# First two attentions of a two-block kernel: values stationary with two heads in column halves, probabilities normalised before they are transposed, four probability buffers

## The reference, cut to what matters

```
s_own = einsum('bhqd,bhkd->bhqk', qc, k_own) * scale        # attention A, 64 features
s_own = where(k_pos <= q_pos, s_own, -inf)
p = softmax(...);  y_a = einsum('bhqk,bhkd->bhqd', p, v)
s = einsum('bhqd,bhkd->bhqk', qb, k) * scale                # attention B, 96 features
p = softmax(where(k_pos <= q_pos, s, -inf));  y_b = einsum('bhqk,bhkd->bhqd', p, v)
merged = sigmoid(gate_a) * (y_a @ w_branch_a) + sigmoid(gate_b) * (y_b @ w_branch_b)
x = x + merged @ w_out
```

## Time and profile before

| | |
|---|---|
| median of 3 runs | 1720.45 us (1718.86 to 1721.94) |
| the profiled execution's own time | 1720.27 us |
| its span (first to last instruction) | 1718.4 us |
| PE busy | 1685.3 us, 98% of the span |
| DVE, ACT, POOL busy | 961.0, 902.1, 1023.5 us |
| the chain that ended last | PE 87%, DVE 4%, ACT 3%, POOL 2% |
| the two attentions | 86.71 to 142.41 us of the span |

### The profile page before, as it was taken

One profiled execution on the slowest core, in us unless ns is written; L12 is line 12 of the kernel. 1 busy time (PEld: TensorE's weight loads), 2 busy tenths in 40 slices (PEclk: granted clock), 3 DMA queues, 4 the chain that ended last, 5 costly groups with the idle time before them and its releaser, 6 DMA issues.

```text
span 1718.4 us, 29498 instructions
## 1 busy us (share of the span) xinstructions
PE 1685.3 (98%) x9320; PEld 1432.7 (83%) x9320; DVE 961.0 (56%) x2062; ACT 902.1 (52%) x1638; POOL 1023.5 (60%) x549
## 2 busy tenths in 40 slices
PE   8999999999999999999999989999999999999998
PEld 7887998888888888888888888888888877788887
DVE  6333489887778885555555557753222266532222
ACT  5565654445444445555445566525555665555554
POOL 4846768888777762000000068627888886578886
PEclk9999999999999999999999999999999999999999
DMA  6634545555544446555655645215555564255553
GB/s 225 177 97 133 203 158 183 183 187 183 166 160 155 157 157 193 191 192 193 195 193 190 224 138 158 74 50 165 187 191 188 179 179 140 85 179 195 186 193 123
DMA packets 83073, 288.18 MB, mean 168 GB/s; under 512 B 9264, under 2 KB 9264, under 8 KB 82480
## 3 DMA queue, kind: packets, MB, share of 16 engines
q1 hardware_dynamic: 82560, 286.10, 51.5%
q10 hardware_dynamic: 432, 1.05, 0.2%
HBM read 285.01 MB, written 2.10 MB: 167 GB/s over the span
## 4 chain that ended last, share of the span: by engine, by line
PE 87%; DVE 4%; ACT 3%; POOL 2%; issue 2%; DMA 1%; DVEq 0%; ACTq 0%; POOLq 0%; SPq 0%
PE acc L652 13%; PE col L955 13%; PE acc L653 13%; PE acc L654 13%; PE col L1249 7%; PE col L957 7%; PE col L1253 4%; POOL w_lo L2022 2%; PE col L689 1%; PE col L690 1%; PE col L691 1%; PE mb L969 1%; PE acc L1168 1%; PE mb L970 1%; ACT w_hi L1465 1%
## 5 line engine op out<-in xcount | busy, mean ns | idle before, releaser
L2022 POOL TENSOR_TENSOR w_lo<-w_raw,w_hi 128x1024 fp32r<-128x1024 f32 (+1 forms) x403 | 952.9, 2380 | 296.7 <-ACT w_hi L1465 274.4
L1465 ACT ACTIVATE w_hi<-w_raw 128x1024 fp32r<-128x1024 f32 (+1 forms) x539 | 565.5, 1052 | 292.1 <-PE acc L654 233.0
L955 PE MATMUL col<-hT,w_hi 128*128 128x512 f32 x1024 | 365.2, 401 | 0.0
L957 PE MATMUL col<-hT,w_lo 128*128 128x256 f32 x1024 | 287.0, 280 | 0.0
L955 PEld LDWEIGHTS col<-hT,w_hi 128*128 128x128 f32 x1024 | 192.4, 188 | 45.7
L652 PE MATMUL acc<-w_hi,W_hi 128*128 128x512 f32 x512 | 199.4, 389 | 0.4 <-ACT W_hi L1686 0.2
L653 PE MATMUL acc<-w_lo,W_hi 128*128 128x512 f32 x512 | 199.2, 389 | 0.0
L654 PE MATMUL acc<-w_hi,W_lo 128*128 128x512 f32 x512 | 199.2, 389 | 0.0
L957 PEld LDWEIGHTS col<-hT,w_lo 128*128 128x128 f32 x1024 | 193.5, 189 | 0.0
L2064 POOL TENSOR_SCALAR_AFFINE_SELECT WST<-WST 128x512 f32<-128x512 f32 x1 | 1.1, 1116 | 319.4 <-DMA WST<-in_gmlp_w 319.4
L2747 DVE TENSOR_TENSOR w_lo<-w_raw,w_hi 128x1024 fp32r<-128x1024 f32 x128 | 156.2, 1221 | 1.3 <-ACT w_hi L1465 1.3
(11 more groups left out here) (589 smaller groups left out, 3070.7 us busy)
## 6 DMA issues: line engine op xcount, KB each, us to landing
w_raw<-in_expert_u SPq DMA_DIRECT2D x128, 512.0 KB, 3.3
w_raw<-in_expert_v SPq DMA_DIRECT2D x128, 512.0 KB, 4.3
w_raw<-in_w_mlp SPq DMA_DIRECT2D x128, 512.0 KB, 3.3
w_raw<-in_w_in SPq DMA_DIRECT2D x24, 512.0 KB, 3.9
w_raw<-in_w_qkv_o SPq DMA_DIRECT2D x24, 512.0 KB, 4.0
w_raw<-in_w_query SPq DMA_DIRECT2D x16, 512.0 KB, 3.3
w_raw<-in_w_gate SPq DMA_DIRECT2D x16, 512.0 KB, 3.4
w_raw<-in_w_qkv_e SPq DMA_DIRECT2D x12, 512.0 KB, 3.8
```

Source lines behind the costliest of these rows:

```text
L955: mm(both, wh[:, k, :], hT[:, :, k, :], start=k == 0, stop=k == KD - 1, skip_group_check=True)
L957: m = mm(both[:, 0, :], wl[:, k, :], hT_hi[:, k, :], start=False, stop=k == KD - 1, skip_group_check=True)
L1465: f(w_hi[:, s, 0:w], w_raw[:, s, 0:w], ACT.Copy).then_inc(sem(f"hi{s}"), 1)
L2022: g.tensor_tensor(w_lo[:, s, 0:w], w_raw[:, s, 0:w], w_hi[:, s, 0:w].bitcast(F32), ALU.subtract).then_inc(sem(f"lo{s}"), 1)
```

## The change

- Values: V of a head (128 tokens x 64 features) is stationary and the transposed probabilities move, 256 columns for key block 0 and 128 for key block 1. Two heads make a pair: the even head writes partitions 0 to 63 of a bank, the odd head 64 to 127. A pair's values are computed in the even turns. The result is features x tokens, so `Y`, `branch_out` and all `y_map` transposes go.
- Normalisation: DVE multiplies `Pr` by the reciprocal of the sums before the transposes (`normed`), one `tensor_tensor` product per query block for each head. PE's transposes wait for it ("probs") where they waited for ACT's exponential.
- `PT` has two buffers of two heads each, instead of one.
- A heads' scores go in pairs, the two heads' matmuls alternating, in the even turns.
- The high and low parts are taken by ACT (`heads_hi`) and DVE (`heads_lo`) straight from `acc[b]`, two pairs at a time; those of B have buffers of their own (`yB_hi`, `yB_lo`).
- The first chunk of br_a waits for its banks one by one. ACT splits gate_b's chunks 2 and 3 a turn or two later than before.

```diff
-        PT = big("PT", 86, [P, 2, 3 * P])
-        Y = big("Y", 90, [P, 2, NT, 8, 64])
+        PT = [big("PT0", 86, [P, 2, 3 * P]), big("PT1_", 106, [P, 2, 3 * P])]
...
-            def scores(u):
-                if u >= 2:
-                    pe.wait_ge(sem("masked"), u - 1)
...
+            def scores(*units):
+                for u in units:
+                    if u >= 2:
+                        pe.wait_ge(sem("masked"), u - 1)
+                    if u >= A_H and u % 2 == 0:
+                        pe.wait_ge(sem("qb_E"), upto("qb_E", u - A_H + 2))
+                for u in units:
+                    q, k = qk_of(u)
+                    mm(col[u % 2][:, 0:P], q[:, 0:P], k[:, 0:P], start=True, stop=True)
+                for u in units:
+                    q, k = qk_of(u)
+                    mm(col[u % 2][:, P:3 * P], q[:, P:2 * P], k, start=True, stop=True).then_inc(
+                        sem("scores"), 1)
...
-            def head_values(u):
...
+            def pair_values(p):
+                b, kk = p % 4 // 2, p % 2
+                pe.wait_ge(sem("pT_E"), upto("pT_E", 2 * p + 2))
+                if p == 0:
+                    pe.wait_ge(sem("ev_kvup"), upto("ev_kvup", 2))
+                if p >= 4 and kk == 0:
+                    pe.wait_ge(sem("yA_E"), b + 1)
+                for kt in range(NT):
+                    for hh in range(2):
+                        h = 2 * p % 8 + hh
+                        v = VC[:, kt, h * 64:(h + 1) * 64] if p < 4 else VB[:, kt, h, :]
+                        o = acc[b][64 * hh:64 * hh + 64, kk * SEQ + kt * P:(kk + 1) * SEQ]
+                        pt = PT[p % 2][:, hh, 0:2 * P] if kt == 0 else PT[p % 2][:, hh, 2 * P:3 * P]
+                        m = mm(o, v, pt, start=kt == 0, stop=kt == 1, skip_group_check=True)
+                m.then_inc(sem("pv"), 1)
...
             for u in range(A_H + B_H):
-                pe.wait_ge(sem("exp"), u + 1)
+                pe.wait_ge(sem("probs"), u + 1)
                 if 5 <= u <= 12:
                     pe.wait_ge(sem("qb_E"), upto("qb_E", u - 4))
-                if 13 <= u <= 14:
-                    pe.wait_ge(sem("yA_E"), upto("yA_E", u - 12))
                 causal_fills(u, Pr[:, u % 2, :], "pT", "pT_E")
-                if u + 2 < A_H + B_H:
+                if u + 2 < A_H:
+                    if u % 2 == 0:
+                        scores(u + 2, u + 3)
+                elif u + 2 < A_H + B_H:
                     scores(u + 2)
-                if u:
-                    head_values(u - 1)
+                if u and u % 2 == 0:
+                    pair_values(u // 2 - 1)
                 if 4 <= u <= 11:
+                    pe.wait_ge(sem("pT_E"), upto("pT_E", u))
                     b_map(u)
-                if 12 <= u <= 13:
-                    y_map(0, u - 12, mb[(u + 1) % 2], "yA_T")
                 gate_b(u)
-            head_values(A_H + B_H - 1)
+            pair_values(A_H - 1)
+            def after_gate_b(t, n):
+                if t:
+                    pe.wait_ge(sem("ev_gb"), upto("ev_gb", 3 + n))
+                else:
+                    pe.wait_ge(sem("yB_E"), n + 1)
...
-                if n >= 2:
-                    act.wait_ge(sem(free), upto(free, n - 1))
-                f(dst[:, n % 2, :], mb[n % 2][:, 0:3 * P], ACT.Copy).then_inc(sem(signal), 1)
+                if n >= 4:
+                    act.wait_ge(sem(free), n // 2 - 1)
+                f(dst[n // 2 % 2][:, n % 2, :], mb[n % 2][:, 0:3 * P], ACT.Copy).then_inc(sem(signal), 1)
+            def heads_hi(m, b, name, pairs):
+                act.wait_ge(sem("pv"), pairs)
+                f(m[:, 2 * b:2 * b + 2, :].rearrange("p k s -> p (k s)"), acc[b][:, :],
+                  ACT.Copy).then_inc(sem(name), 1)
...
-                if u == 1:
-                    split_to(FIRST["gb"] + 4)
+                if u in (1, 2):
+                    split_to(FIRST["gb"] + 1 + u)
...
+                if u in (5, 9):
+                    heads_hi(yA_hi, (u - 5) // 4, "yA_H", (u - 1) // 2)
+                if u == 13:
+                    heads_hi(yB_hi, 0, "yB_H", 6)
             copy_probs(0, PT, "pT", "pv", A_H + B_H - 1, "pT_E")
             gate_b(1)
+            heads_hi(yB_hi, 1, "yB_H", 8)
             split_to(FIRST["br_a"] + 4)
-            stream_hi("y", range(2))
...
+            def normed(u):
+                dve.wait_ge(sem("exp"), u + 1)
+                then(v.reciprocal(sums[:, u, :], sums[:, u, :]))
+                for t, (a, b) in enumerate(((0, P), (P, 3 * P))):
+                    p = Pr[:, u % 2, a:b]
+                    i = v.tensor_tensor(p, p, sums[:, u, t:t + 1].to_broadcast([P, b - a]), ALU.mult)
+                    if t == 0:
+                        go(i)
+                i.then_inc(sem("probs"), 1)
...
                 masked(Sm[:, u % 2, :], col[u % 2], causal, mx[:, u, :], "masked")
+                if u:
+                    normed(u - 1)
...
+                if u in (8, 12):
+                    heads_lo(yA_hi, yA_lo, (u - 8) // 4, "yA_H", "yA_E")
+            normed(A_H + B_H - 1)
+            for b in range(2):
+                heads_lo(yB_hi, yB_lo, b, "yB_H", "yB_E")
```

More of the change, by code:

```diff
@@ L352, in program @@
         QTA = big("QTA", 40, [P, 8, SEQ])
[L353 to L354 removed]
+        yB_hi = big("yB_hi", 40, [P, 4, SEQ], F32R)
+        yB_lo = big("yB_lo", 44, [P, 4, SEQ], F32R)
         QB = big("QB", 48, [P, NT, B_H, B_DK])
@@ L645, in row_chunk @@
                         second_half()
-                    if t == 0 and n == 0 and t0_freed:
-                        pe.wait_ge(sem(t0_freed[0]), upto(*t0_freed))
+                    if bank_free:
+                        bank_free(t, n)
                     a, b = splits_of(j)[n]
@@ L821, in b_map @@
                 m.then_inc(sem("qb_T"), 1)
[L823 to L831, removed]
             def gate_b(u):
@@ L854, in gate_b @@
                     m.then_inc(sem(f"used{s}"), 1)
-            scores(0)
-            scores(1)
+            scores(0, 1)
             row_group("kvup", "ev_qup", *from_c(2))
             for u in range(A_H + B_H):
-                pe.wait_ge(sem("exp"), u + 1)
+                pe.wait_ge(sem("probs"), u + 1)
                 if 5 <= u <= 12:
                     pe.wait_ge(sem("qb_E"), upto("qb_E", u - 4))
-                if 13 <= u <= 14:
-                    pe.wait_ge(sem("yA_E"), upto("yA_E", u - 12))
@@ L873, in _ @@
                     b_map(u)
-                if 12 <= u <= 13:
-                    y_map(0, u - 12, mb[(u + 1) % 2], "yA_T")
                 gate_b(u)
-            head_values(A_H + B_H - 1)
[L880 to L886, removed]
-            for k in range(4):
[L888 to L894, removed]
+            pair_values(A_H - 1)
@@ L895, in _, with of @@
+            def after_gate_b(t, n):
[3 more added lines that the diff above has]
+                    pe.wait_ge(sem("yB_E"), n + 1)
+            def of(m):
+                return lambda k: lambda t: m[:, k, t * P:(t + 1) * P]
+            pe.wait_ge(sem("yA_E"), 2)
+            for k in range(4):
+                row_chunk(FIRST["br_a"] + k, 0, of(yA_hi)(k), of(yA_lo)(k), k == 0, k == 3,
                           order=(1, 0) if k == 0 else range(NT),
-                          t0_freed=("y", 4) if k == 0 else None)
@@ L2424, in masked, with heads_lo @@
                 i.then_inc(sem(name), 1)
-            def branch_out(br):
-                dve.wait_ge(sem("exp"), 8 * br + 8)
-                then(v.reciprocal(sums[:, 8 * br:8 * br + 8, :], sums[:, 8 * br:8 * br + 8, :]))
-                dve.wait_ge(sem("pv"), 8 * br + 8)
-                for t in range(NT):
-                    then(v.tensor_tensor(Y[:, br, t, :, :],
-                                         acc[t][:, :].rearrange("p (h d) -> p h d", h=8),
-                                         over(sums[:, 8 * br:8 * br + 8, t], [P, 8, 64], 2),
-                                         ALU.mult), "y")
+            def normed(u):
[7 more added lines that the diff above has]
+                i.then_inc(sem("probs"), 1)
+            def heads_lo(hi, lo, b, name, done):
+                dve.wait_ge(sem(name), upto(name, b + 1))
+                k = slice(2 * b, 2 * b + 2)
+                v.tensor_tensor(lo[:, k, :].rearrange("p k s -> p (k s)"), acc[b][:, :],
+                                hi[:, k, :].bitcast(F32).rearrange("p k s -> p (k s)"),
+                                ALU.subtract).then_inc(sem(done), 1)
             dve.wait_ge(sem("causal"), 3)
```

46 lines of the change are left out of this document (9 added, 37 removed).

## The result

| | median (range), us | against before |
|---|---|---|
| before | 1719.57 (1718.86 to 1721.94, 11 runs) | |
| after | 1725.03 (1722.59 to 1727.47, 11 runs) | 1.0031, 95% interval 1.0022 to 1.0039 |
| predicted | 1713.0 (1710.6 to 1718.6) | |

The changed kernel is slower by 0.31%, 5.5 us, where 7.4 us less were forecast. The forecast started from 1720.45, a median of 3 runs; from the 1719.57 of 11 runs, 7.4 less is 1712.2. The rival that had the smallest chance has come true: DVE's products are held by POOL.

What follows compares the result with a forecast made beforehand. PE was taken to bound the kernel (busy 98% of the span). PE work 9.03 less, plus 0.80 for Y's transposes, minus 2.4 of new waits, made 7.4 less: from 1720.45 to 1713.0, range 1710.6 to 1718.6.

Steps and rivals of the forecast that it cites:

- the third rival: DVE's normalising products stand until POOL's low parts end: 11 us held in all, kernel slower at 1724; chance 0.06.
- the two held lines of the earlier trace: DVE instructions L2410 and L3141, held by POOL's w_lo: 2.51 beside 0.32 usual, 2.19 beside 0.22.
- the point of decision: Held DVE products decide the outcome from 7.4 us on, seven of the ten.
- Ten low parts at 1.1 each: In the two attentions, each POOL low part holds one head's product for 1.1 on average: 11 us.
- The pieces on PE: PE's transposes, scores, values, map and gate_b over the two attentions: sum 46.67 against 55.70 before, 9.03 less.
- serial halves: Values' column halves run one after the other, 1.53 a pair instead of 0.87: gain 2.1, time 1718.3; chance 0.15.
- the rule of the Trainium skill: On PE, a weight load overlaps running matmuls only if the row group differs; value pairs would go towards the serial price.
- The new waits: PE waits for DVE's new step: 0.59 in each of turns 7, 9, 11, 0.29 in turn 14, 0.3 at the start; 2.4.
- The late chain: Exponential, product, evacuation late in nearly every turn; turn 3's margin 0.07; 0.3 a head costs 4.8: 1717.8; chance 0.11.
- the tail behind the loop: After the loop, heads_hi and heads_lo end about 2.0 after the last values; covered by br_a's first chunk within 0.2.
- the 0.80 of the Y maps: Behind the two attentions, the 8 transposes of Y of B, about 0.1 each, go: 0.80 less.

## Why the prediction was wrong

- **The step that failed** is the argument against the third rival: "L2747 is a plain two-source product, all SBUF, beside POOL's w_lo, 1219 in the median and 1319 at most over 128 times", and from it "The held ones are of two other operations". The row is right, the words "beside POOL's w_lo" are not. L2747 is DVE's share of the low parts, at 646 to 990 us, and POOL has none there, as a window of the kernel before with the w_lo tiles alone shows:

```profile
core 0: us, POOL busy (x), PEclk, DMA share, GB/s
646.00:990.00 344.00, 0.00 (x0) 1.00 0.60 197
```

  So 128 unhurried products proved nothing, and the two held lines of the earlier trace rows, which did lie beside low parts, were set aside as exceptions. The rival had the mechanism, the place and the point of decision (7.4 us held); it got a chance of 0.06 on this reading. The other one against it, the reciprocal L3140, is right but says nothing of a product: reciprocals weren't held here either (0.16 inside a low part), products were.
- **Its size.** Ten low parts at 1.1 each made 11 us, and 1724. Measured: seven heads at 2.05 on average, 14.4 us, and 0.4 by `rope_t` on head 0; 1725.03. Fewer heads and more a head than I had: in five of the seven the product and a low part start within 0.4 us of one another. Not all reaches PE (13.6 us of waits, 11.2 beyond the 2.4 forecast). That 1724 comes so near is partly luck.
- **The pieces on PE** held. A pair of values takes 0.80 (forecast 0.87) whichever way it is queued, a pair of scores 0.86 (0.87). The serial halves (1.53) didn't come about, so the rule of the Trainium skill that the prediction set against it (TensorE: Matmul & The Clock Gate, The mechanism: loads overlap only if the row group differs) did not show here: both heads' loads fill the same rows, and the pair takes 0.80, near the 0.66 that the prediction's sum has for one head's columns and far from the 1.32 for two.
- **The new waits** apart from the hold: 2.4 forecast, 2.0 measured with the low parts cut, counted from start to start. They are 0.46, 0.55 and 0.45 before turns 8, 10 and 12 (0.59 each), 0.30 before turn 1 (0.3) and 0.25 before turn 14 (0.29). The profile's brackets show 0.28 to 0.39 for the first three and nothing for the others. One term was missing: the first transposes come 0.34 later (87.05 for 86.71), ahead of this sum, behind head 0's product that `rope_t` holds.
- **The late chain** in turn 3 and the tail behind the loop: neither appears. With the holds gone or mostly gone the stretch is 48.93 to 50.37 in four kernels, 49.07 forecast. Their medians, 1712.5 to 1713.3, are 6.4 to 7.2 under the kernel before that ran beside each (7.4 forecast).
- **After the stretch**: the 0.80 of the Y maps came (22.69 for 23.60). The profile of the changed kernel also has 3.4 us at the lower clock level behind the merge (granted clock 0.94 from 170.44 to 199.00, matmuls 0.43 apart instead of 0.23), which cost it 1.6. PE had stood idle for 0.62 and 0.98 us shortly before; the kernel with the squared product has the same two idles and kept its clock. From 170.44 to its end it takes 1552.9, where the kernel before takes 1552.4 from the same place, so 4.4 of the 4.9 us that its span is longer had come before the fall. The two kernels with the product in another form have the same holds and a clock of 1.00 there, and their spans are 1722.1 and 1722.0 for 1723.3. So that fall doesn't belong to every execution and isn't the cause of the loss; whether it has a share in the median of the changed kernel stays open.

## What to carry to other kernels

Before an instruction is put on DVE beside POOL's long ones, look where its operands lie: with all of them in SBUF it can stand until the POOL instruction ends, with an input in PSUM it did not. If such a step lies on the path, start POOL's work behind it (here one wait, 7 us, and 12 with the product moved ahead of the mask) or move that work; how often they meet isn't given by POOL's share of time, since both may be released by the same engine. And a row that is to prove that two things don't disturb each other proves it only if both ran at that time: open the window of the second engine first.

## What the runs showed of the hardware

- A held product ends just behind the POOL instruction, 0.15 us for 128 columns and 0.28 for 256, whenever it began: 128 columns of 0.29 took 0.71 to 2.44 in the changed kernel, 256 columns of 0.42 took 2.59 and 2.60. A reciprocal of 128x2 inside the same low parts stayed at 0.16.
- The reverse is small: low parts that start together with a product take 2.52 to 2.53 instead of 2.37 to 2.39, and a POOL instruction of 0.73 beside head 0's second product takes 1.00.
- Two heads in the column halves run together in either queueing order: 0.80 and 0.81 for a pair of 2 x (256 + 128) columns in fp32.
- A wait added to POOL made the kernel 7.1 us faster: in neither profile does PE wait for one of the low parts from 84 to 250 us, so the work held back was early.
